# Forgetting attention's scores in a two-block transformer kernel: from plain F32 products to two fp32r products of split parts

## The reference

```
h = rms_norm(x, g_norm)
q, k, v, fl, gf, u, gs, qm, gm, gl = split_cols(h @ w_in)
log_f = log_sigmoid(fl + b_forget)            # one value for each row and head
F = cumsum(log_f)                             # over the 512 rows
S[h, i, j] = q[i, h] . k[j, h] / 8 + F[i, h] - F[j, h]    for j <= i
y = softmax(S) @ v                            # then times silu(gf)
```

## Time and profile before

| | |
|---|---|
| timed runs | 1987.69, 1986.69, 1985.87 us, median 1986.69 |
| profiled execution, span | 1984.3 us (no time of its own is listed beside its span) |
| PE busy | 1939.3 us, 98% |
| DVE, ACT, POOL busy | 1080.7, 898.4, 876.9 us (54%, 45%, 44%) |
| the attention with its scores | from 1386 to 1590 us of the span |

### The profile page before, as it was taken

One profiled execution on the slowest core, in us unless ns is written; L12 is line 12 of the kernel. 1 busy time (PEld: TensorE's weight loads), 2 busy tenths in 40 slices (PEclk: granted clock), 3 DMA queues, 4 the chain that ended last, 5 costly groups with the idle time before them and its releaser, 6 DMA issues.

```text
span 1984.3 us, 28065 instructions
## 1 busy us (share of the span) xinstructions
PE 1939.3 (98%) x11059; PEld 1590.2 (80%) x11059; DVE 1080.7 (54%) x1802; ACT 898.4 (45%) x1713; POOL 876.9 (44%) x672
## 2 busy tenths in 40 slices
PE   5999999999999999999999999999999999999998
PEld 4868887888788877888888888888788778888886
DVE  5577879694466646664544440345765576511114
ACT  3555656564455544233434342344555454422223
POOL 1323333234533326564444444454474461655542
PEclk9999999999999999999999999999999999999999
DMA  8255353543322117664332334336123223433331
GB/s 308 73 167 181 114 185 118 181 137 108 98 70 57 43 45 289 226 225 159 96 105 87 106 89 142 99 116 187 51 76 84 78 61 104 159 98 95 89 109 72
DMA packets 92323, 242.43 MB, mean 122 GB/s; under 512 B 28192, under 2 KB 31392, under 8 KB 90784
## 3 DMA queue, kind: packets, MB, share of 16 engines
q1 hardware_dynamic: 88784, 231.98, 37.2%
q10 hardware_dynamic: 3408, 8.65, 1.1%
HBM read 223.14 MB, written 14.29 MB: 120 GB/s over the span
## 4 chain that ended last, share of the span: by engine, by line
PE 92%; DVE 2%; ACT 2%; SPq 1%; DMA 1%; POOL 1%; issue 1%; ACTq 0%; DVEq 0%
PE ps L943 23%; PE ps L944 23%; PE ps L952 22%; PE ps L1273 3%; PE ps L1348 2%; PE ps L1335 2%; PE ps L1410 1%; PE ps L1323 1%; PE ps L1250 1%; PE ps L1007 1%; PE ps L1014 1%; PE ps L1008 1%; DMA modwb<-in_w_mod 1%; PE ps L947 1%; PE ps L1233 1%; PE ps L1429 1%
## 5 line engine op out<-in xcount | busy, mean ns | idle before, releaser
L2843 POOL TENSOR_TENSOR wlo<-raww,whi 128x512 fp32r<-128x512 f32 x207 | 281.1, 1358 | 687.1 <-ACT whi L1475 686.6
L1475 ACT CAST whi<-raww 128x1024 fp32r<-128x1024 f32 (+2 forms) x279 | 279.4, 1006 | 173.5 <-PE ps L952 146.9
L2844 POOL TENSOR_TENSOR wlo<-raww,whi 128x512 fp32r<-128x512 f32 x207 | 286.4, 1384 | 0.0
L943 PE MATMUL ps<-hT_h,whi 128*128 128x512 f32 (+1 forms) x688 | 252.7, 377 | 1.2 <-ACT whi L1475 0.6
L944 PE MATMUL ps<-hT_l,whi 128*128 128x512 f32 (+1 forms) x688 | 245.5, 366 | 0.0
L943 PE MATMUL ps<-H_h,whi 128*128 128x512 f32 x480 | 189.5, 395 | 0.6 <-DVE sq L2075 0.4
L944 PE MATMUL ps<-H_l,whi 128*128 128x512 f32 x480 | 187.1, 390 | 0.0
L952 PE MATMUL ps<-hT_h,wlo 128*128 128x512 f32 (+1 forms) x688 | 152.0, 363 | 0.0
L943 PEld LDWEIGHTS ps<-hT_h,whi 128*128 128x128 f32 x688 | 130.5, 190 | 25.9 <-issue 3.4
L944 PEld LDWEIGHTS ps<-hT_l,whi 128*128 128x128 f32 x688 | 130.5, 190 | 22.3 <-issue 1.9
L952 PEld LDWEIGHTS ps<-hT_h,wlo 128*128 128x128 f32 x688 | 119.3, 189 | 20.3
(11 more groups left out here) (590 smaller groups left out, 4421.0 us busy)
## 6 DMA issues: line engine op xcount, KB each, us to landing
ec<-csd SPq DMA_DIRECT2D x32, 1024.0 KB, 8.0
raww<-in_w_up SPq DMA_DIRECT2D x44, 512.0 KB, 3.6
modr<-in_w_mod SPq DMA_DIRECT2D x32, 512.0 KB, 5.9
raww<-in_w_xbc SPq DMA_DIRECT2D x24, 512.0 KB, 3.8
raww<-in_w_gl SPq DMA_DIRECT2D x24, 512.0 KB, 3.6
raww<-in_w_z SPq DMA_DIRECT2D x16, 512.0 KB, 3.8
raww<-in_w_g SPq DMA_DIRECT2D x16, 512.0 KB, 3.6
raww<-in_w_os SPq DMA_DIRECT2D x16, 512.0 KB, 3.9
```

Source lines behind the costliest of these rows:

```text
L943: e.matmul(o, whi[:, i, c], hi(k)[:, t0:t1], start=(k == 0), stop=False)
L1475: e.copy(o, x.rearrange("p (k c) -> p k c", c=64) if p == plan.first["dt", 0] else x).then_inc(*w_high.mark(("high", p)))
L2843: e.tensor_tensor(o[:, 0:512], x[:, 0:512], h[:, 0:512].bitcast(F32), ALU.subtract).then_inc(*p_wlow.mark(("first half", p)))
L2844: e.tensor_tensor(o[:, 512:1024], x[:, 512:1024], h[:, 512:1024].bitcast(F32), ALU.subtract).then_inc(*p_wlow.mark(("split", p), ("raw fre ...
```

## The change

The scores are made of fp32r parts. For each head `qk` now has four pictures of 128 rows: Q_STACK (rows 0 to 63 q/8 rounded to fp32r, rows 64 to 127 what the rounding left), K_TWICE (k rounded, twice), Q_HIGH (q/8 rounded in rows 64 to 127, rows 0 and 1 ones) and K_LOW (k's rest in rows 64 to 127, rows 0 and 1 the high and low part of F). Two fp32r products, Q_STACK by K_TWICE and Q_HIGH by K_LOW, give q.k up to the product of the two rests.

Each head has a product with weights of its own (`fq h`, 64 columns of q beside 64 of k, by another order of the columns of `w_fqk`), 12 in all as before. `fqout h` is now four instructions of ACT and two of DVE, and the bank is given back only when both have marked it. A new step `frows` rounds the sums F on ACT, takes the rest on DVE and starts the DMAs. `head_by_head` rewrites the order: fq 0 and fq 1 stand ahead of the values, u 5 moves behind them, and gf 3 and the qm move later. The buffers `qk` have one place for the even and one for the odd heads.

```diff
+def head_by_head(o):
+    heads = {0: 0, 6: 1, 7: 2, 2: 3, 8: 4, 3: 5, 9: 6, 4: 7, 10: 8, 5: 9, 11: 10}
+    out = []
+    for s in o:
+        if s in (("u", 5), ("fqout", 1), ("gf", 3), ("gfout", 3), ("qm", 1), ("qmout", 0), ("qmout", 1), ("qmout", 2)):
+            continue
+        if s == ("fq", 1):
+            out.append(("u", 5))
+        elif s[0] in ("fq", "fqout"):
+            out.append((s[0], heads[s[1]]))
+            if s == ("fq", 0):
+                out.append(("frows",))
+        else:
+            out += {("qm", 0): [("fq", 11), ("fqout", 11), ("gf", 3), ("gfout", 3)], ("qm", 2): [("qm", 0), ("qmout", 0), ("qm", 1), ("qmout", 1)],
+                    ("qm", 3): [("qm", 2), ("qmout", 2), s]}.get(s, [s])
+    return out
...
-        fqk = lambda h, i: qk[:, h // 2 % 2, 2 * i + h % 2, :]
+        fqk = lambda h, i: qk[:, h % 2, i, :]
+        Q_STACK, Q_HIGH, K_TWICE, K_LOW = 0, 1, 2, 3
...
-                        e.matmul(ps[:, b, a:a + Wd], fqk(h, 0)[:, i * 128:(i + 1) * 128], fqk(h, 1)[:, 0:Wd], start=True, stop=False)
+                        e.matmul(ps[:, b, a:a + Wd], fqk(h, Q_STACK)[:, i * 128:(i + 1) * 128], fqk(h, K_TWICE)[:, 0:Wd], start=True, stop=False)
+                        e.matmul(ps[:, b, a:a + Wd], fqk(h, Q_HIGH)[:, i * 128:(i + 1) * 128], fqk(h, K_LOW)[:, 0:Wd], start=False, stop=False)
...
+                    e.mul(fqk(h, Q_STACK)[0:64, :], ps[0:64, b, :], 0.125).then_inc(*x_high.mark())
+                    e.mul(fqk(h, Q_HIGH)[64:128, :], ps[0:64, b, :], 0.125).then_inc(*x_high.mark(("fq high", h)))
+                    e.copy(fqk(h, K_TWICE)[64:128, :], ps[64:128, b, :]).then_inc(*x_high.mark())
+                    e.copy(fqk(h, K_TWICE)[0:64, :], ps[64:128, b, :]).then_inc(*x_high.mark(("fk high", h), ("out of", (src, 0))))
+                elif k == "frows":
+                    ACTE.wait_ge(at("forget sums"))
+                    e.copy(FT[0:12, :], ffs[:, 2, :]).then_inc(*x_high.mark(("forget high",)))
...
+                elif k == "frows":
+                    DVE.wait_ge(at("forget high"))
+                    e.tensor_tensor(FT[32:44, :], ffs[:, 2, :], FT[0:12, :].bitcast(F32), ALU.subtract).then_inc(*v_made.mark(("forget rows",)))
+                elif k == "fqout":
+                    h, src = s[1], ("fq", s[1])
+                    b = bank_of((src, 0))
+                    DVE.wait_ge(at("fq high", h))
+                    e.scalar_tensor_tensor(out=fqk(h, Q_STACK)[64:128, :], in0=ps[0:64, b, :], scalar=0.125, in1=fqk(h, Q_STACK)[0:64, :].bitcast(F32),
+                                           op0=ALU.mult, op1=ALU.subtract).then_inc(*v_xlow.mark())
+                    DVE.wait_ge(at("fk high", h))
+                    e.tensor_tensor(fqk(h, K_LOW)[64:128, :], ps[64:128, b, :], fqk(h, K_TWICE)[64:128, :].bitcast(F32), ALU.subtract).then_inc(
+                        *v_xlow.mark(("fq low", h), ("out of", (src, 0))))
```

More of the change, by code:

```diff
@@ L1402, in tensor_program @@
                         b = bank(s, OLDEST)
-                        PE.wait_ge(at("fq", h // 2))
-                        PE.wait_ge(at("fq", 6 + h // 2))
+                        PE.wait_ge(at("fk high", h))
+                        PE.wait_ge(at("fq low", h))
                         PE.wait_ge(at("forget row", h))
@@ L2882, in pool_program @@
                     after_last()
-                    e.memset(qk[64:128, :, :, :].rearrange("p a b c -> p (a b c)"), 0.0).then_inc(*p_step.mark())
+                    for h in (0, 1):
+                        e.memset(fqk(h, Q_HIGH)[0:64, :].bitcast(F32), 0.0).then_inc(*p_step.mark())
+                        e.memset(fqk(h, K_LOW)[0:64, :].bitcast(F32), 0.0).then_inc(*p_step.mark())
                     after_last()
-                    for i in (0, 1):
-                        e.memset(qk[64:65, i, 0:2, :].rearrange("p b c -> p (b c)"), 1.0).then_inc(*p_made.mark(*[("rows of ones",)] * i))
+                    for h in (0, 1):
+                        e.memset(fqk(h, Q_HIGH)[0:2, :].bitcast(F32), 1.0).then_inc(*p_made.mark(*[("rows of ones",)] * h))
                         after_last()
@@ L3151, in sync_program @@
                             *y5_out[m % 2].mark(*[("y5 stored", m)] * (t == 7)))
[L3152 to L3156, removed]
+                elif k == "frows" or k == "fqout" and s[1] >= 2:
+                    if k == "frows":
+                        SP.wait_ge(at("forget rows"))
                         SP.wait_ge(at("rows of ones"))
-                    if k == "forget" or 0 < m < 6:
-                        for h in (2 * m, 2 * m + 1):
-                            if h >= 4:
-                                SP.wait_ge(at("fscores", h - 4, 3))
-                            e.dma_start(fqk(h, 1)[64:65, :], FT[h:h + 1, :]).then_inc(*f_row[h % 4].mark(("forget row", h)))
+                    for h in (0, 1) if k == "frows" else (s[1],):
+                        if h >= 2:
+                            SP.wait_ge(at("fscores", h - 2, 3))
+                        for i in (0, 1):
+                            e.dma_start(fqk(h, K_LOW)[i:i + 1, :].bitcast(F32), FT[32 * i + h:32 * i + h + 1, :].bitcast(F32)).then_inc(
+                                *f_row[h % 4].mark(*[("forget row", h)] * i))
                 elif k == "yin":
@@ L3231 @@
     w = I["w_in_2"][0]
-    arr["w_fqk"] = blocks(w[:, 0:1536])
+    arr["w_fqk"] = blocks(_np.concatenate([w[:, 0:768].reshape(1024, 12, 64), w[:, 768:1536].reshape(1024, 12, 64)], axis=2).reshape(1024, 1536))
     arr["w_fv"] = wide(w[:, 1536:2304])
```

20 lines of the change are left out of this document (8 added, 12 removed).

## The result

The changed kernel takes 2011.99 us (median of four runs, 2011.88 to 2013.72) against 1986.95 us: a ratio of 1.013, 95% interval 1.0118 to 1.0142, so 25 us slower. The profiled execution took 2012.08 us with a span of 2010.4, 26.1 us above the span of the earlier trace rows.

A forecast was written before the change was run, and what follows sets the result against it. PE was taken to bound the kernel; 8.7 + 1.7 + 5.2 + 0.8 + 1.0 - 3.0 = +14.4 us took the 1984.3 span to 1998.7, and 2.4 more gave 2001.1 us. Range: 1991 to 2008, eight in ten.

The forecast's parts named there:

- The first wait: Ahead of the first values, PE stands still 8.7 us until DVE's rests free fq 0's bank; bounds 5.8 to about 10.
- the half clock behind it: After the stop ahead of the first values, the granted clock falls to half: +1.7 us, bounds 0 and 1.7.
- DVE's block from the fill of `Tp` to that of `Hp`: DVE work ahead of head 0's rests: takes 9.04 us, with three slow operations as in the earlier timeline.
- The new rests: DVE's two rests per head, each reading one PSUM input: 0.69 us each, about 1.5 if held up by the lock.
- Heads 0 to 4: Up to the second values: they start 5.2 us later, savings counted in, plus 0.8 for half a clock fall.
- The saving for each head: PE's score products: 2.22 us in F32 against 1.26 plus 0.06 in fp32r, saving 0.9 a head, 10.8 for 12.
- Heads 5 to 8 ... Net +1.0: Heads 5 and 6 save 1.8 us; waits of about 1.25 (head 5) and 1.6 (head 7) leave a net +1.0.
- Heads 8 to 11 save 0.9 us each with nothing new behind them: Last heads keep their savings except part of head 8: -3.0 us.
- score waits put down to ACT's exp: Sign of being wrong: exp instead of DVE's rest releases score waits, so the softmax chain, not the bank, sets the pace.
- a last stretch that is not shorter by 0.9 a head: Sign of being wrong: from head 9 to the end, the saving of 0.9 us a head does not appear.
- (c): Rival: every wait of some 2 us costs a clock fall, +20.3 us in all, 2007.0 us; chance 0.25.
- the likeliest case: Whole-kernel forecast of +14.4 us, bounds -2.9 - 2.5 and +1.3 + 1.7, so 1995.7 to 2004.1 us.

The follow-up runs named there:

- e5: Changed kernel without DVE's two rests per head, so scores lack the low parts of q and k: 1995.57 us, ratio 1.0042.
- e6_nohelp: As e5, and ACT makes only two of the four copies per head; order and two fp32r products stay: 1988.20 us, ratio 1.0013.
- e13_nohelp_f32: e6_nohelp with one plain F32 product per score instead of two fp32r ones, row of F left out: 1990.45 us, ratio 1.0027.
- e4: Changed kernel with one plain F32 product per score, Q_STACK by K_TWICE, instead of two fp32r ones; K_LOW left out: 2011.67 us, ratio 1.0125.
- e2: Changed kernel with group 2's scan of S5 and making of Hp moved ahead of head 11's rests and gf 3 on DVE: 2006.68 us, 1.0102.
- e7: Changed kernel with edits of e1_first and e2, plus ACT's copies reordered to give the bank back at the second: 1996.19 us, ratio 1.0053.
- e9: Changed kernel with edits of e1_first and e2, three fp32r products of rows 0 to 65 per score, two ACT copies per head: 2003.69 us, 1.0090.
- e10: Kernel before, own order, with fp32r qk and one fp32r product per score; low parts of q and k left out: 1984.28 us, ratio 0.9991.
- e14: e6_nohelp with softmax's last step on ACT scaling only the first 32 columns of each P: 1986.30 us, ratio 1.0003.
- e1_first: Changed kernel with head 0's copies and rests right behind the fill of Tp, head 1's between the halves of bbar: 2005.52 us, ratio 1.0097.

## Why the prediction was wrong

**The direction and the first terms held.** The first wait was forecast at 8.7 and is 7.00; the half clock behind it at 1.7 and is 2.5 (F, 19.5 against 17.0). DVE's block from the fill of `Tp` to that of `Hp` was slowed once (1.51) and not three times: it took 7.24 us, not 9.04. The new rests took 0.69 us each time, as priced. Two rows of the changed kernel, all instructions of each line:

```profile
L2729 DVE SCALAR_TENSOR_TENSOR qk<-ps,qk x12: 683/684/685, 1370.9 to 1564.8; 64x512 fp32r<-64x512 f32 x12
...
L2732 DVE TENSOR_TENSOR qk<-ps,qk x12: 694/694/695, 1371.6 to 1566.0; 64x512 fp32r<-64x512 f32 x12
```

The rule of the Trainium skill, page "SBUF — State Buffer", section "SBUF: two separate sides", names operations of DVE with two SBUF inputs (against an operation of GpSimd that reads SBUF) or in a 2-port mode as those that wait for GpSimd; these have one input in PSUM, and the rows agree: ten of the 24 ran while POOL worked on tiles of SBUF, and none took over 0.695 us.

Heads 0 to 4 were forecast at 5.2 + 0.8 = 6.0 and took 6.2. This is in part luck. The waits at the 512 columns of heads 1 and 2 stand where they were put, but at 1.59 and 1.19 for 1.6 and 2.1. The turned P of head 0 waits 0.38 for 0.7, those of heads 1 and 2 not at all. Not forecast were the 1.22 for an exp at 1405.55 with a whole fall of the clock behind it, and 0.9 more for DVE's `sq` at 1434.00.

**The saving for each head was right in sum.** The prediction read the x2 of the earlier trace rows as two products with the mask in them. They are the two records of one F32 product, without the mask (start to start 0.27 and 0.22 us at 256 columns); the cost of 2.22 us a head is right all the same. PE's timeline of the changed kernel, two products and the mask at 128 and at 512 columns:

```profile
1492.07 0.22 PE L1430 MATMUL ps<-qk 128*128 128x128 f32 x1
1492.12 0.28 PE L1431 MATMUL ps<-qk 128*128 128x128 f32 x1
1492.24 0.23 PE L1432 MATMUL ps<-maskb 128*128 128x128 bf16 x1
1494.02 0.48 PE L1430 MATMUL ps<-qk 128*128 128x512 f32 x1
1494.34 0.40 PE L1431 MATMUL ps<-qk 128*128 128x512 f32 x1
1494.57 0.23 PE L1432 MATMUL ps<-maskb 128*128 128x128 bf16 x1
```

From the start of the first product to that of the mask it is 0.17 and 0.55 us, where I had 0.22 and 0.45 (and 0.06 of cover lost for all widths); at 128 columns it is up to 0.28 in other places. A head's scores went from 2.43 to 1.72 us with the mask, 0.7 less; the turned P between them, 7 of which went from 0.77 to 0.69, bring it to some 0.9.

**The step that failed is "Heads 5 to 8 ... Net +1.0" and "Heads 8 to 11 save 0.9 us each with nothing new behind them".** B lost 6.3, 5.3 more than forecast. I had counted two waits there, 1.25 and 1.6; the trace has them (0.76 and 1.97). Left out were the waits for exp, 1.26 and 1.12, and the half clock, 1.4 us behind the second values and 1.7 at 1497 to 1501. The maxima that the exp of the first needs stand behind the rests in DVE's list, and without rests the wait is 0.61 (e5). The 1.12 has nothing to do with them. The same wait in before, in e6_nohelp and in e13_nohelp_f32:

```profile
1501.88 0.50 PE L943 MATMUL ps<-H_h,whi 128*128 128x512 f32 x1 [0.25 <-ACT Pf L1510]
1495.40 0.50 PE L963 MATMUL ps<-H_h,whi 128*128 128x512 f32 x1 [1.12 <-ACT Pf L1531]
1495.74 0.50 PE L963 MATMUL ps<-H_h,whi 128*128 128x512 f32 x1 [0.26 <-ACT Pf L1530]
```

With F32 products it is 0.25 or 0.26 (e4 too), with fp32r products 1.12, helpers busy or not: PE is done with one head's scores 0.87 us sooner and waits that much longer for the same exp. This is a saving being eaten, seen directly, and the wait at 1434.00 is another (1.22, and 0.36 in before, e4 and e13). e5 and e6 show that the net loss of B comes with the rests and copies: without them B is 0.9 shorter than before. The step also set 1.8 us of saving for heads 5 and 6 against the waits; e13 against e6 shows 0.9 for all four heads even with idle helpers, and e4 shows less than nothing with them.

C lost 2.6 where 3.0 were to be gained. With the scan moved back, C is 80.1 in e2 and 79.2 in four kernels that have other edits too, 2.3 to 3.2 less than before. So the saving of the last heads fits (no run has F32 products with the scan moved back), and 4.9 (e2) to 5.8 (e7) of the miss of 5.6 us are the scan of S5 behind the gate. I had read the change's lists at fq 0, at head 1 and at the banks, and not at the place where `gf 3` and `fq 11` moved past the scan on DVE, though the rule that a moved step carries its instructions past each queue was the one to apply.

The prediction named both as signs of being wrong: score waits put down to ACT's exp, and a last stretch that is not shorter by 0.9 a head.

The rest is 1.5 us of chance ahead of the first values. Together: -0.9 (first wait and clock) + 0.2 + 5.3 + 5.6 + 1.5 = 11.7, the 26.1 measured less the 14.4 forecast. The rival that came nearest was (c), more falls of the clock, at 2007.0; the four falls that it put behind the first one happened (at 1405, 1450, 1497 and 1575), but it lacked the wait for the scan. The upper bound of the likeliest case added 1.7 for falls of which 0.9 was left; nothing hangs on it.

**What holds PE between first and third values** is shown only in part. That product time is hidden there is shown from four sides (e4, e9, e10, e13): e13 against e6, with equal helpers, keeps 1.7 us of the nine heads' 7.8. That DVE's and ACT's lists do it follows from e5 and e6. Of what they hold, softmax's scaling is 0.7 and 0.4 us (e14). The rest, DVE's powers of S5 ahead of head 3's maxima above all, is read from the timelines and was not tried. Nor was the clock held apart: each price of a stretch holds the falls that came with it.

## What to carry to other kernels

A saving on the busiest engine counts only as far as that engine meets nobody else's late work; before counting it, find for each stretch who would be met first. Work added to helpers must be costed as delay of what stands behind it in their list, not as share of busy time: here two rests of 0.7 us a head on a DVE busy 54% cost 7.8 us over heads 0 to 8, about 0.9 for each head. When steps are moved, go through every in-order list they pass, for a moved step that waits (a gate's output here) holds up work that needs nothing of it.

## What the runs showed of the hardware

Three products of 64 or 66 rows were not cheaper each than two of 128 rows, but dearer. In e9 the next product starts after 0.32 to 0.34 us at 512 columns and after 0.16 to 0.20 at 128. In the changed kernel the first of two 128-row products of 512 columns takes 0.32 to the next start and the second 0.23, as `1494.02` and `1494.34` show; at 128 columns it is 0.06 to 0.17 and 0.12. Whether the row count, the change between row counts or the loads cost this was not separated.

The granted clock fell to 0.50 behind the waits of 7.00, 3.09 and 3.99 us, behind that of 1.93 ahead of head 3's scores (in before too), and behind two pairs of shorter waits, 1.59 and 1.22 at 1403 to 1405 and 0.76 and 1.26 at 1495 to 1497. It did not behind the wait of 1.97 at 1528.52: the 24 products of 256 columns behind it took 2.98 us, as in before (2.95), and the clock was 1.00. Behind the same wait of 1.97 in e1_first and e2_scan it was 0.52. So the length of one wait does not tell in these runs whether the clock falls.
